# Products of probabilities and values, issued once per group of four units

## What is computed

```python
def masked_softmax(s, mask):
    s = jnp.where(mask, s.astype(jnp.float32), NEG_INF)
    m = jnp.max(s, axis=-1, keepdims=True)
    e = jnp.where(mask, jnp.exp(s - m), 0.0)
    return e / jnp.maximum(jnp.sum(e, axis=-1, keepdims=True), 1e-30)
...
    s = jnp.einsum('bqkgd,bskd->bkgqs', qb, kw) * SCALE
    p = masked_softmax(s, mask)
    return jnp.einsum('bkgqs,bskd->bqkgd', p.astype(vw.dtype), vw)
```

## Time and profile before

| what | us |
|---|---|
| median of three runs | 942.88 |
| span of the profiled execution | 942.1 |
| PE busy | 907.5 (96%) |
| DVE busy | 520.0 (55%) |
| ACT busy | 414.2 (44%) |
| POOL busy | 291.1 (31%) |
| PE on the chain that ended last | 79% of the span |

### The profile page before, as it was taken

How to read it: one execution, slowest core, us unless ns; L and a number is a source line. 1 busy time by engine, 2 the same in 40 slices (tenths; PEclk the granted TensorE clock), 3 DMA queues, 4 the chain that set the end, 5 groups by cost and what they waited for, 6 DMA issues and landing times.

```text
span 942.1 us, 20736 instructions
## 1 busy us (share of the span) xinstructions
PE 907.5 (96%) x7830; PEld 825.0 (88%) x7830; DVE 520.0 (55%) x1302; ACT 414.2 (44%) x1063; POOL 291.1 (31%) x495
## 2 busy tenths in 40 slices
PE   6999999999999999999999999999999999999997
PEld 6999999999999999999988788868887787878885
DVE  5656332323225476545656687676677758844443
ACT  6443221234343101221656666565765657932221
POOL 0223222212214444544253162325222625410000
PEclk9999999999999999999999999999999999999999
DMA  8654422404240544232878068715504142333331
GB/s 231 177 193 135 143 84 109 160 30 121 71 149 23 141 125 141 67 104 71 213 201 202 7 185 259 240 44 150 148 2 140 47 140 75 105 132 137 126 122 67
DMA packets 85076, 118.10 MB, mean 125 GB/s; under 512 B 12914, under 2 KB 67234, under 8 KB 84402
## 3 DMA queue, kind: packets, MB, share of 16 engines
q1 hardware_dynamic: 71522, 73.30, 27.1%
q0 software_dynamic: 10224, 36.20, 11.7%
q10 hardware_dynamic: 3232, 7.28, 2.1%
HBM read 91.68 MB, written 32.02 MB: 131 GB/s over the span
## 4 chain that ended last, share of the span: by engine, by line
PE 79%; DVE 6%; ACT 4%; issue 4%; DMA 2%; POOL 2%; SPq 2%; ACTq 0%; DVEq 0%; POOLq 0%
PE psum L593 8%; PE psum L594 7%; PE psum L595 7%; PE psum L1866 7%; PE psum L1742 6%; PE psum L1715 4%; PE psum L1885 3%; PE psum L1886 3%; PE psum L1887 3%; PE psum L1716 3%; PE psum L834 2%; PE psum L836 2%; PE psum L835 2%; PE psum L817 2%; PE psum L580 2%
## 5 line engine op out<-in xcount | busy, mean ns | idle before, releaser
L593 PE MATMUL psum<-a_whi,f_xhi 128*128 128x256 f32 (+1 forms) x672 | 194.5, 289 | 1.6 <-DVE f_xlo L1059 1.4
L594 PE MATMUL psum<-a_wlo,f_xhi 128*128 128x256 f32 (+1 forms) x672 | 190.3, 283 | 0.0
L595 PE MATMUL psum<-a_whi,f_xlo 128*128 128x256 f32 (+1 forms) x672 | 189.7, 282 | 0.0
L1975 ACT ACTIVATE p_P<-psum,p_nb 128x640 f32<-128x640 f32 (+7 forms) x224 | 124.2, 561 | 41.3 <-DVE p_nb L2043 37.9
L2043 DVE TENSOR_REDUCE p_nb<-psum 128x1 f32<-128x640 f32 (+7 forms) x224 | 110.4, 523 | 50.9 <-PE psum L1716 43.5
L593 PEld LDWEIGHTS psum<-a_whi,f_xhi 128*128 128x128 f32 x672 | 127.1, 189 | 4.1 <-DVE a_wlo L569 1.8
L595 PEld LDWEIGHTS psum<-a_whi,f_xlo 128*128 128x128 f32 x672 | 127.1, 189 | 0.0
L594 PEld LDWEIGHTS psum<-a_wlo,f_xhi 128*128 128x128 f32 x672 | 127.1, 189 | 0.0
L736 POOL DMA_DIRECT2D h_scratch<-a_hst x93 | 51.3, 554 | 213.7 <-DVE a_hst L1120 104.5
L1742 PE MATMUL psum<-f_ident,p_P 128*128 128x128 f32 x656 | 98.9, 275 | 1.6 <-DVE p_PT L1913 0.9
L1742 PEld LDWEIGHTS psum<-f_ident,p_P 128*128 128x128 f32 x656 | 77.1, 141 | 7.6 <-DVE p_PT L1913 2.2
(11 more groups left out here) (335 smaller groups left out, 2137.2 us busy)
## 6 DMA issues: line engine op xcount, KB each, us to landing
a_wraw<-in_w_in SPq DMA_DIRECT2D x24, 512.0 KB, 4.2
h_scratch<-a_hst POOLq DMA_DIRECT2D x72, 128.0 KB, 3.5
s_SG<-in_cache_nsa_slc SPq DMA_DIRECT2D x64, 128.0 KB, 2.1
p_qd<-q_scratch SPq DMA_DIRECT2D x16, 384.0 KB, 7.8
a_xraw<-in_x_prompt SPq DMA_DIRECT2D x8, 512.0 KB, 6.9
s_MK<-in_cache_mem SPq DMA_DIRECT2D x8, 512.0 KB, 9.0
s_WG<-in_cache_nsa_win SPq DMA_DIRECT2D x8, 512.0 KB, 4.5
mix_scratch<-p_zt POOLq DMA_DIRECT2D x8, 512.0 KB, 3.4
```

The lines of the kernel that those rows point to most:

```text
L593: nc.tensor.matmul(out, hi, wh, start=first, stop=False)
L594: nc.tensor.matmul(out, hi, wl, start=False, stop=False)
L595: return nc.tensor.matmul(out, lo, wh, start=False, stop=last)
L1975: nc.scalar.activation(dst, s_view(s), ACT.Exp, bias=nb[:, g % NNB:g % NNB + 1], accum_out=ssum[:, par[i], s[1]:s[1] + 1]).then_inc(S("p_e ...
```

## The change

- A burst is issued only where a new block begins: after the transposes of its first unit come all products of the block before, in one go (56 instructions for the largest tile). At the end the rest follows behind the first output tile, as before.
- The eight buffers become three segments of 20, 12 and 7 columns of 128 (`PTA`, `PTB`, `PTC`). `place_probabilities()` walks the steps when the kernel is built, gives each chunk a free stretch of just its width, and notes how many product steps must be over before the copy may write there (`pt_after`). The third segment lies in the sample group's region.
- `gf` moves onto the memory keys `KM`, and its load on SP moves from before the first load of mixed rows to behind the wait for the last scores.

```diff
--- before.py
+++ after.py
@@ -257,8 +257,7 @@
 
     NNB = 6
     NC = 64
-    NPT = 8
-    NPT0 = 5
+    NPTA, NPTB, NPTC = 20, 12, 7
     rp = Region(nc, arena, "p_")
     split_at = rp.at
     QA = [rp(f"QA{i}", [128, 12, 128], F32R) for i in range(2)]
@@ -274,7 +273,7 @@
     zt = [rp(f"zt{i}", [128, D]) for i in range(2)]
     gt = [rp(f"gt{i}", [128, 24]) for i in range(2)]
     pt_at = rp.at
-    PTs = [rp(f"PT{i}", [128, 512]) for i in range(NPT0)]
+    PTA = rp("PTA", [128, 128 * NPTA])
     assert rp.at >= z_at, (rp.at, z_at)
     qd1_at = rp.at
     qd1 = rp("qd1", [128, 12, 128])
@@ -288,12 +287,13 @@
     KW = rp("KW", [128, 2, NC + T + NC], F32R)
     v_at = rp.at
     V = rp("V", [128, 2, QT, 128])
+    km_at = rp.at
     KM = rp("KM", [128, 4, NM], F32R)
     VM = rp("VM", [128, 2, 256])
     rk = Region(nc, rp.at, "pk_")
     Ktok = rk("Ktok", [128, 2, QT, 128])
     Kmt = rk("Kmt", [128, 2, 256])
-    PTs += [rp(f"PT{i}", [128, 512]) for i in range(NPT0, NPT)]
+    PTB = rp("PTB", [128, 128 * NPTB])
     OT = rp("OT", [128, 384])
     Oi = [rp(f"Oi{i}", [128, 6, HD]) for i in range(2)]
     assert rk.at <= rp.at <= LIMIT, (rk.at, rp.at, LIMIT)
@@ -342,6 +342,7 @@
     gs = ru("gs", [NS_TOK, 24])
     on_s = ru("on_s", [NS_TOK, 8, 3, HD])
     om_s = ru("om_s", [NS_TOK, 4, HD])
+    PTC = ru("PTC", [128, 128 * NPTC])
     assert ru.at <= ident_at, (ru.at, ident_at)
 
 
@@ -349,7 +350,7 @@
     dwraw = [rd(f"wraw{i}", [128, 4, 512]) for i in range(2)]
     dwhi = [rd(f"whi{i}", [128, KT, 512], F32R) for i in range(2)]
     dwlo = [rd(f"wlo{i}", [128, KT, 512], F32R) for i in range(2)]
-    gf = rd("gf", [128, D])
+    gf = nc.alloc_sbuf_tensor_at("d_gf", [128, D], F32, offset=km_at)
     assert rd.at <= ident_at, (rd.at, ident_at)
     mt = [nc.alloc_sbuf_tensor_at(f"d_mt{i}", [128, D], F32, offset=at) for i, at in enumerate((qd0_at, qd1_at))]
     rd = Region(nc, split_at, "d_")
@@ -1474,7 +1475,7 @@
                 elif l % 2:
                     waiting.append((partner[len(mine) - 1], mine[-1]))
             partner = mine
-            while waiting and (l % 2 == 0 or l >= 16) and waiting[0][1] not in mine:
+            while v and unit_block[v] != unit_block[v - 1] and waiting and waiting[0][1] not in mine:
                 pv()
             if v + 2 < NV:
                 steps.append(("sm", v + 2))
@@ -1543,18 +1544,46 @@
 
     place = {c: k for k, c in enumerate(p_chunks) if c[0] != "p"}
     p_index = [k for k, c in enumerate(p_chunks) if c[0] == "p"]
-    p_rank = {c: n for n, c in enumerate(p_index)}
     last_chunk = {p_chunks[c][1]: c for c in p_index}
     x_last = {c[1]: k for k, c in enumerate(p_chunks) if c[0] == "x"}
     split_rank = {c: n for n, c in enumerate([k for k, c in enumerate(p_chunks) if c[0] == "x"])}
 
-    pv_freed, ot_pv, n_pv = {}, {}, 0
-    for what, n in p_steps:
-        if what == "pv":
-            n_pv += 1
-            pv_freed.update({c: n_pv for c in n})
-        elif what == "ot":
-            ot_pv[n] = n_pv
+    pt_segs = [(PTA, NPTA), (PTB, NPTB), (PTC, NPTC)]
+
+    def place_probabilities():
+
+        freed = [[0] * n for _, n in pt_segs]
+        spot, after, first, done, n_pv = {}, {}, set(), {}, 0
+        for what, n in p_steps:
+            if what == "t" and p_chunks[n][0] == "p":
+                w = len(p_chunks[n][2])
+                runs = []
+                for s, seg in enumerate(freed):
+                    for at in range(len(seg) - w + 1):
+                        if None not in seg[at:at + w]:
+                            left = next((k for k in range(at, 0, -1) if seg[k - 1] is None), 0)
+                            right = next((k for k in range(at + w, len(seg)) if seg[k] is None), len(seg))
+                            runs.append((right - left - w if at == left else 99, max(seg[at:at + w]), s, at))
+                _, wait, s, at = min(runs)
+                spot[n], after[n] = (s, at), wait
+                if 0 in freed[s][at:at + w]:
+                    first.add(n)
+                freed[s][at:at + w] = [None] * w
+            elif what == "pv":
+                n_pv += 1
+                for c in set(n):
+                    s, at = spot[c]
+                    freed[s][at:at + len(p_chunks[c][2])] = [n_pv] * len(p_chunks[c][2])
+            elif what == "ot":
+                done[n] = n_pv
+        return spot, after, first, done
+
+    pt_spot, pt_after, pt_first, ot_pv = place_probabilities()
+
+    def pt_view(c, w, j, n):
+
+        s, at = pt_spot[c]
+        return pt_segs[s][0][0:w, 128 * (at + j):128 * (at + j + n)]
 
     def s_view(s):
 
@@ -1648,7 +1677,6 @@
                 if n == 0:
                     sp.wait_ge(S("p_qs"), 3 * (QT - 1))
                     sp.wait_ge(S("s_mxo"), 16)
-                    sp.dma_start(gf[:], io["ln_final"].rearrange("(o n) -> o n", o=1).to_broadcast([128, D])).then_inc(S("d_const"), 16)
                 if n >= 2:
                     sp.wait_ge(S("p_tr"), x_last[n - 2] + 1)
                 sp.wait_ge(*mix_done(t))
@@ -1657,6 +1685,7 @@
                 t = D_ORDER[n]
                 if n == 0:
                     sp.wait_ge(S("p_qk"), NV)
+                    sp.dma_start(gf[:], io["ln_final"].rearrange("(o n) -> o n", o=1).to_broadcast([128, D])).then_inc(S("d_const"), 16)
                 if n >= 2:
                     sp.wait_ge(S("d_sum"), 2 * (n - 1))
                 sp.dma_start(xr[n % 2][0:tile_rows(t)], x_rows[t]).then_inc(S(f"d_x{n % 2}"), 16)
@@ -1863,7 +1892,7 @@
                     at = 512 * 7 + 128 * ((num - numbers(num // 6).start) // 2)
                     kv = HD * (h // 4)
                     val = VM[:, k, HD * h:HD * h + HD] if b == 3 else VC[0:w, NDB, kv:kv + HD] if b == 2 else V[:, b, k0 + k, kv:kv + HD]
-                    i_mm = nc.tensor.matmul(psum[64 * j:64 * j + 64, at:at + 128], val, PTs[p_rank[pair[j]] % NPT][0:w, 128 * p:128 * p + 128],
+                    i_mm = nc.tensor.matmul(psum[64 * j:64 * j + 64, at:at + 128], val, pt_view(pair[j], w, p, 1),
                                             start=k == 0, stop=128 * (k + 1) >= keys, skip_group_check=True)
             i_mm.then_inc(S("p_pv"), 1)
 
@@ -1902,15 +1931,15 @@
     def pt_copy(eng, copy, c, sem):
 
         n, w = len(p_chunks[c][2]), max(t[2] for t in p_chunks[c][2])
-        r = p_rank[c]
+        s, at = pt_spot[c]
         eng.wait_ge(S("p_tr"), c + 1)
-        if r < NPT0:
+        if c in pt_first and s == 0:
             for b in range(HST):
-                if hst_at + 4 * WMAX * b < pt_at + 2048 * (r + 1) and pt_at + 2048 * r < hst_at + 4 * WMAX * (b + 1):
+                if hst_at + 4 * WMAX * b < pt_at + 512 * (at + n) and pt_at + 512 * at < hst_at + 4 * WMAX * (b + 1):
                     eng.wait_ge(S(f"h_out{b}"), 16 * len(range(b, len(proj_jobs), HST)))
-        if r >= NPT:
-            eng.wait_ge(S("p_pv"), pv_freed[p_index[r - NPT]])
-        copy(PTs[r % NPT][0:w, 0:128 * n], bank(4 + c % 3)[0:w, 0:128 * n]).then_inc(sem, 1)
+        if pt_after[c]:
+            eng.wait_ge(S("p_pv"), pt_after[c])
+        copy(pt_view(c, w, 0, n), bank(4 + c % 3)[0:w, 0:128 * n]).then_inc(sem, 1)
 
     def sample_copy(eng, copy, c, sem):
 
```

## The result

The changed kernel takes 950.53 us in the median of four runs (950.35 to 953.13), the kernel before 943.24 in four (942.88 to 944.38): ratio 1.0076, 95% interval 1.0061 to 1.0091. Repeated in a later set with more runs it is 1.0071, 1.0058 to 1.0084. So it is slower by about 7 us, beyond the 0.2% that can be told from no change. The execution shown is the longest of the four, 953.13 us.

What follows compares the result with a forecast made beforehand. PE was taken to set the pace, with little left on ACT and DVE at the end. Terms of -2.97 and +4.22 us gave +1.25 us on the 942.88 us median: 944.1 us, range 938.5 to 951.0, own range 941 to 948.

Steps and rivals of the forecast that it cites:

- the second rival: Attention stage: ACT becomes the pace, exponentials wait behind the OT copy; slower, 948.0 or 951.8 us; chance 0.35.
- Part 1, the switches: Attention stage, PE: joining bursts cuts form changes 168 to 106, saves 0.24 us per joined burst, 7.0 us in 29 blocks.
- Part 2, the cushion: Attention stage: waits after the moved burst lose its cover; 14 blocks gain 2.97 us, 10 nothing, 14 lose 4.22 us.
- the rule: Per block: slack above moved burst's length plus 0.24 us gains 0.24; below, gains slack less that length, possibly negative.
- the first rival: Attention stage: waits shrink as DVE catches up and stalls vanish; faster, 940.2 us, or 935.9 if no block lost; chance 0.24.
- Parts 3 and 4: Chunk copies waiting for freed buffer columns, and the last norm's weights loaded later on SP's queue: each predicted to cost nothing.
- Its clause on sample-group products and their waits: Argument for slower: sample-group products behind the moved burst, whose waits were not followed, come earlier too; no size given.
- What would show it: Signs: 40 bursts, idle loads about half of 69, ACT's wait up most of 33.6 us, exponential waits mostly after 790 us.

Runs made afterwards that it cites:

- the spare products: Kernel before with a spare product in 104 product steps: 997.26 us in 128 columns, 962.33 us in 64 columns.
- the repeat: The changed kernel unaltered, measured again on the same chip as a later set: 951.91 us, ratio 1.0071.
- experiment 1: Changed kernel with the old order of two bursts per block; new buffers and moved load stay: 945.27 us, ratio 1.0006.
- experiment 7: Changed kernel with five late copies of transposed probabilities made by DVE instead of ACT: 949.92 us, ratio 1.0049.
- experiment 5: Changed kernel with ten blocks keeping their two bursts, the other 30 joined: 947.46 us, ratio 1.0021.
- experiment 9: Kernel before with a spare 64-column product in 104 product steps, so no form changes: 962.33 us, ratio 1.018.
- experiment 2: Changed kernel with exponentials of unit v+2 issued ahead of the burst and OT copy: 950.34 us, ratio 1.0055.
- 8: Kernel before with a spare 128-column product in 104 bursts of 64-column products: 997.26 us, ratio 1.0548.
- 10: Changed kernel with only eleven blocks joined, all others keeping two bursts: 943.57 us, ratio 0.9987.
- 12: Only seven blocks joined, plus four copies of transposed probabilities swapped between ACT and DVE: 941.45 us, ratio 0.9953.
- 1 to 6: Includes two runs not named singly: kernel before with exponentials ahead of the burst, 945.25 us; changed kernel with only block 30 keeping two bursts, 951.03 us.
- 11: Kernel before with four copies of transposed probabilities swapped between ACT and DVE, nothing else: 943.54 us, ratio 0.998.

## Why the prediction missed

The forecast was 944.1 us and no measurable difference; it became 950.5, slower by 0.76%. The number lies in the range (938.5 to 951.0), but only 0.5 us from its end and outside the forecast's own 941 to 948: it is the width given to the second rival that covers it, not the forecast's sum.

**Part 1, the switches: right.** 0.24 us per joined burst was read from one burst; blocks with nothing late gain 0.25 to 0.26, and the idle loads went from 69 to 32. The 0.34 of the spare products is another place, inside a burst.

**Part 2, the cushion: right in its mechanism, wrong in its list.** "The same was done for the copies three chunks back" held for chunks of probabilities and of OT only. The sample group's chunks use the same three banks, and the text had said of them that their waits were not followed. That is the step that failed. For the ten blocks of the table the working had -1.07 us, and +6.1 were measured; 2.5 of these 7.2 us of difference are block 30's. In the ten blocks nine of the new waits stand ahead of a sample-group instruction, and the tenth ends with the copy of a sample chunk; over the stage such waits of sample-group instructions for copies grew from 4.1 us to 9.1. Where it did follow the wait, it was close: (1, 2) 0.43 and measured 0.44, (1, 3) 0.41 and 0.43, (1, 1) 0.12 and 0.13, (6, 1) 0.26 and 0.22. It erred among the followed ones too: (6, 3) had 0.84 and measured 0.48, (3, 2) 0.37 and 0.02, (3, 4) 0.37 and 0.05, (4, 2) 0.52 and 0.91 (0.38 in the repeat). Three gained more than 0.24, which the rule does not allow: (0, 4) with 0.66, (2, 2) with 0.58 and (2, 3) with 0.35. In (0, 4), where this was followed, waits that existed before became shorter, as the first rival had it: 0.30 and 1.22 us are 0.05 and 0.79 in the changed kernel.

**A term that was absent: the clock.** No step allowed for a stall that costs again afterwards. At block 30 it added about 1.3 us. By the prediction's own rule the wait at 754.21 has no slack, so this block would have stood at +1.09 instead of -0.24; with the clock's 1.3 that is 2.4, and 2.28 were measured.

**Parts 3 and 4: right**, nothing each, by experiment 1.

**The second rival** had the time (948.0 to 951.8) and half of the cause. That exponentials behind the waiting OT copy set the pace is not borne out: with that wait cut to 20.1 us the joined order kept most of its loss, and PE's waits for exponentials grew by 2.1 us against 5.0 for copies ahead of the sample group. Its clause on sample-group products and their waits was the part that decided. I had listed it as an argument for a rival and given it no price; two windows of the trace of before, at 637.53 and 754.21 us, showed PE waiting there 1.22 and 1.05 us already, at exactly such transposes.

**What would show it:** the growth of the loads' waits for exponentials was expected mostly after 790 us. It came before: from 7.2 to 13.0 us up to there, and only 2.7 in 6 places after. Waits for copies on PE's load side, the sign that parts of this would fail, stood in no line of that list.

**What stays open.** The experiments show the copies in block 30 (experiment 7) and that ten blocks hold two thirds of the loss; for the other nine the cause is read from the profile, as in (7, 0), where PE waits 0.65 us for a copy that stands behind a sample exponential of 0.78, and was not tried one by one. The shares of 5.0 us for copies and 2.1 for exponentials are waits as the profile assigns them; an earlier copy could leave PE waiting for the exponential behind it. Why (0, 4) gains only beside joined neighbours was not tried either; the traces show that with neighbours split (experiment 5) a wait of 0.70 us for a copy stands ahead of its OT transposes, where the changed kernel has 0.05.

## What to carry to other kernels

A block of work that does not wait, such as these products, is a cushion for whatever follows it on an in-order engine. Before it is moved, list *every* wait behind it up to its new place, the small side stream's too, with the slack of each; an existing stall there is the warning, since the cushion's length is added to it (1.05 us became 2.29). And the largest growing wait of another engine (ACT's +30 us) says little: read what the bounding engine waits for, where a copy of 0.58 us behind long exponentials held it for 2.29 us, and one line moved such copies to the engine that was free at that moment.

## What the runs showed of the hardware

A stall of TensorE can cost again by the clock. All three profiled executions with the 2.29 us stall at block 30 had a stretch at 0.50, the 1.2 GHz level, that began between 0.1 us before the stall's end and 1.4 us after it; neither the kernel before nor experiment 7, with 1.05 and 0.89 us there, had one. It is not fixed by the stall alone: PE stood for 2.31 us at 42.3 us in experiment 9, and for 1.39 us at 623.0 us in experiment 2, and the clock stayed up. At 306 us, ahead of the attention stage, every profiled execution stalls for 1.82 or 1.83 us:

```profile
306.02 0.38 PE L581 MATMUL psum<-f_xhi,a_whi 128*128 128x256 f32 x1 [1.82 <-DVE a_hst L1119]
```

Here the changed kernel's shown execution ran at the lower clock from about 307.0 to 310.5 us, and those of experiments 7, 8, 10 and 12 for as long; the kernel before and experiments 1 to 6, 9 and 11 kept full speed. The same 60 instructions behind the stall took 8.5 us in those five executions and 7.0 in the other nine, so one such stretch costs 1.5 us here. That fits the spread of one kernel's times: nine runs of experiment 2 go from 946.9 us at a mean clock of 0.999 to 953.3 at 0.993. It is why single differences of 2 us were judged here by blocks of the trace.

The Trainium skill (TensorEngine Tiling (Array Packing), Key Properties) says that a change of tiling mode drains the engine. The trace agrees in that every change shows a gap (products start 0.20 us after the last transpose, where product follows product after 0.055), and the runs give it a price here: 0.25 us for a pair at the edges of a burst, 0.34 inside one.
